# A two-layer streaming encoder: the depthwise convolution of its third mixer moved from taps on ScalarE and GpSimd to block-diagonal matmuls on TensorE

## The chip, the cores and the metric

The kernel runs on one core of a Trainium2 chip. The metric is the device time of one execution in microseconds (us). Before the change it is 3272.25 us, the median of three runs (3271.8 to 3272.7).

## The reference, cut to what matters

Two batches go through the same two layers: 1024 prompt tokens, and 32 sampled tokens with a cache of 2048 past keys. The model width is 1024. A layer is:

```python
h = rmsnorm(x, g_norm1[l]) * (1.0 + sc1) + sh1
z = h @ w_in[l]                      # 2116 columns, shared among three mixers
a_out = gmlp(za)     # gelu; v standardised in groups of 64 channels; 128x128 causal mixing; times u
b_out = sparse(...)  # indexer scores, the best 256 keys of each query kept, attention over them
c_out = conv(zc)
x = x + ga1 * (concatenate([a_out, b_out, c_out]) @ w_out[l])
h2 = rmsnorm(x, g_norm2[l]) * (1.0 + sc2) + sh2
x = x + ga2 * ((silu(h2 @ w_gate[l]) * (h2 @ w_up[l])) @ w_down[l])

def conv(zc):                        # 256 channels, 31 taps
    a, g = split(zc)
    hp = concatenate([state_or_zeros, a * sigmoid(g)])
    y[t, ch] = sum(hp[t + tap, ch] * w_dw[tap, ch] for tap in range(31)) + b_dw[ch]
    return silu(group_standardize(y, 4) * g_cn)
```

## The kernel before, in words

Everything is kept channel by partition: a tensor of 1024 channels is eight blocks of 128 partitions by 1056 tokens (1024 prompt, 32 sampled). The five engines run written-out programs in order and meet only at semaphores.

A weight strip is 1024 by 128. SP loads it into `w_raw` (L381), ScalarE rounds it to `w_hi` (`split_hi`, L579), GpSimd makes the rest `w_lo` (`split_lo`, L503), and TensorE does 72 matmuls of 352 columns with it (`strip`, L817): eight blocks of the input, three products each, three pieces of the tokens. Two triples of PSUM banks take turns; banks 6 and 7 are free for work beside the strips.

A layer begins with the norm. Then 17 input strips follow. VectorE rotates the queries and keys (`rotate`, L1221), four vector instructions per strip; ScalarE copies the others out. Beside strips 4 to 6 the indexer scores are made. Then the best 256 keys of each query are found by a bitwise threshold search of 31 rounds (`candidates` L1260, `decide` L1271). In one round VectorE counts three of the six score rows and ScalarE the other three (`count`, L621), and VectorE waits for ScalarE before it keeps or drops the bit. The rounds are spread over the strips by the table `SEARCH_AFTER`, and each engine runs them after its other work of that strip. In this order the convolution's and the gMLP's strips are the last eight (9 to 16). They do not fit in memory, so they are spilled to DRAM and read back.

After the strips comes a stretch that is called the gate here: gMLP's v is standardised, transposed, mixed by `w_spatial`, multiplied by u. Standardising is a mean matmul, `centre` (L1325), a squaring, a variance matmul, `deviation` (L636: logarithm and exponential) and `scale` (L1330). `finish_search` and the first `select` (L1303) run on VectorE beside it.

Then comes attention, for eight blocks i of 128 queries. TensorE makes the logits of block i+1 (`logits`, L975), then for each key block of block i the transposed scores (`st`, L991) and the product with the values (`pv`, L1008). VectorE takes maxima and writes the next `select`; ScalarE does the exponentials (`exponentials`, L719). A second search of 31 rounds, for the sampled tokens, runs in here too: some rounds in the maxima (`SEARCH_IN`), some beside the exponentials (`SEARCH_BESIDE`).

The convolution also runs here. For each of the 2 x 31 taps ScalarE multiplies the padded input `hp` by one weight per partition into `ctmp` (`tap`, L700) and GpSimd adds it to `cy` (L531). Its mean and variance follow after the sampled tokens' attention (L1088 to L1101), then SiLU, and the output projection of eight strips.

## Time and profile before

The profiled execution took 3274.92 us; its span, from the first to the last instruction, is 3273.0 us.

| stretch (us from the start) | what runs | length | TensorE busy |
|---|---|---|---|
| 0 to 140 | modulation weights, first norm, first strip | 140 | 88.1 |
| 140 to 401 | input strips of layer 0 | 261 | 229.8 |
| 401 to 437 | gate | 36 | 19.2 |
| 437 to 770 | attention and convolution | 333 | 257.1 |
| 770 to 870 | output projection | 100 | 95.3 |
| 870 to 1624 | feed-forward | 754 | 734.8 |
| 1624 to 3273 | layer 1, and the last norm | 1649 | 1449.9 |

The engines are busy 88% (TensorE), 50% (VectorE), 35% (ScalarE) and 25% (GpSimd) of the span. The table is a first guide only: an engine's busy share is an average over stages with different limits, so each stage is read by itself, above all by who waits for whom.

### The profile page before, as it was taken

What the parts mean: (1) busy time and instruction counts of PE and PEld (TensorE: products, weight loads), DVE (VectorE), ACT (ScalarE), POOL (GpSimd) and SP (SyncE); (2) the same over time, 40 slices, a digit from 0 to 9 for tenths busy, and PEclk for the clock granted to TensorE, in tenths of its full rate; (3) what the DMA queues carried; (4) which work ended last, traced back from release to release, by engine and by line L of the source; (5) the groups of instructions that cost most, each with busy time, mean ns of one, the idle gap of its engine ahead of it and who ended that gap; (6) DMA issues with size and microseconds to landing.
All of it is one profiled execution on the core that took longest, in us unless ns stands there. A gap on an engine that the chain in (4) does not pass through costs nothing.

```text
span 3273.0 us, 42010 instructions
## 1 busy us (share of the span) xinstructions
PE 2874.0 (88%) x15770; PEld 2472.4 (76%) x15770; DVE 1620.5 (50%) x2488; ACT 1139.7 (35%) x1338; POOL 815.1 (25%) x340
## 2 busy tenths in 40 slices
PE   6699576788799999999979966678889999999996
PEld 6679432238799999999967863223689999999996
DVE  7668667743433232433455875765324424333244
ACT  1327747733411111111242574684323111111113
POOL 0111127711122222222211102772011222222221
PEclk9999788899899999999989987899899999999998
DMA  9212200010122122222211230001011212222222
GB/s 350 85 40 75 103 2 0 1 33 26 45 92 72 63 89 69 83 77 71 78 59 50 69 116 2 0 1 33 20 52 71 84 64 81 67 96 68 74 82 79
DMA packets 70242, 214.49 MB, mean 66 GB/s; under 512 B 17280, under 2 KB 17536, under 8 KB 69120
## 3 DMA queue, kind: packets, MB, share of 16 engines
q1 hardware_dynamic: 67504, 202.71, 18.3%
q10 hardware_dynamic: 2640, 10.49, 0.8%
q8 instruction: 60, 0.98, 0.1%
q14 instruction: 38, 0.31, 0.0%
HBM read 196.76 MB, written 15.87 MB: 65 GB/s over the span
## 4 chain that ended last, share of the span: by engine, by line
PE 64%; DVE 14%; ACT 9%; issue 6%; DVEq 2%; DMA 2%; POOL 1%; ACTq 1%; SPq 0%; POOLq 0%
PE ps L825 56%; ACT notsel L626 4%; DVE smax L1443 2%; DMA w_ada<-in_w_ada 2%; PE ps L1015 1%; PE ps L854 1%; DVE s_keep L1274 1%; POOL cy L531 1%; PE ps L983 1%; DVE w_ada L1155 1%; DVE junk L1155 1%; ACT ctmp L710 1%; DVE notsel L1322 1%; DVE notsel L1319 1%; DVE score L1314 1%
## 5 line engine op out<-in xcount | busy, mean ns | idle before, releaser
L505 POOL TENSOR_TENSOR w_lo<-w_raw,w_hi 128x1024 fp32r<-128x1024 f32 x202 | 497.3, 2462 | 2184.8 <-ACT w_hi L586 2184.8
L825 PE MATMUL ps<-h_hi,w_hi 128*128 128x352 f32 x2928 | 648.2, 330 | 62.0 <-DVE h_lo L1143 48.4
L825 PE MATMUL ps<-h_lo,w_hi 128*128 128x352 f32 x2928 | 634.7, 325 | 0.0
L825 PE MATMUL ps<-h_hi,w_lo 128*128 128x352 f32 x2928 | 634.7, 324 | 0.0
L825 PEld LDWEIGHTS ps<-h_hi,w_hi 128*128 128x128 f32 x2928 | 499.6, 191 | 106.0 <-issue 78.1
L825 PEld LDWEIGHTS ps<-h_hi,w_lo 128*128 128x128 f32 x2928 | 505.7, 189 | 0.0
L825 PEld LDWEIGHTS ps<-h_lo,w_hi 128*128 128x128 f32 x2928 | 501.9, 189 | 0.0
L586 ACT CAST w_hi<-w_raw 128x1024 fp32r<-128x1024 f32 x202 | 211.3, 1046 | 642.5 <-PE ps L825 443.0
L531 POOL TENSOR_TENSOR cy<-cy,ctmp 128x1086 f32<-128x1086 f32 x120 | 303.5, 2529 | 229.2 <-ACT ctmp L710 224.4
L626 ACT ACTIVATE notsel<-score,s_cand 128x384 bf16<-128x384 f32 (+3 forms) x248 | 297.2, 1199 | 152.7 <-DVE s_cand L1262 152.5
L1547 DVE TENSOR_TENSOR act_f<-silu,ps 128x1056 f32<-128x1056 f32 x44 | 55.2, 1254 | 595.4 <-PE ps L825 595.4
L1530 DVE SCALAR_TENSOR_TENSOR x<-ps,mod,x 128x704 f32 (+2 forms) x240 | 125.4, 578 | 400.8 <-PE ps L825 394.8
L1155 DVE SCALAR_TENSOR_TENSOR junk<-w_ada,cond_row 128x1024 f32<-128x1024 f32 x124 | 243.7, 1965 | 33.3 <-issue 23.7
L825 PE MATMUL ps<-a_hi,w_hi 128*128 128x352 f32 x1056 | 227.8, 324 | 0.7 <-DVE x L1530 0.7
L825 PE MATMUL ps<-a_hi,w_lo 128*128 128x352 f32 x1056 | 227.5, 323 | 0.0
L825 PE MATMUL ps<-a_lo,w_hi 128*128 128x352 f32 x1056 | 227.0, 323 | 0.0
L794 ACT CAST a_hi<-act_f 128x1056 f32 x44 | 47.3, 1076 | 485.7 <-DVE act_f L1547 485.7
L1015 PE MATMUL ps<-probs,vaug 128*128 128x512 f32 x288 | 151.2, 655 | 70.9 <-ACT probs L724 70.9
L825 PEld LDWEIGHTS ps<-a_hi,w_lo 128*128 128x128 f32 x1056 | 180.8, 188 | 0.0
L825 PEld LDWEIGHTS ps<-a_hi,w_hi 128*128 128x128 f32 x1056 | 179.6, 189 | 1.3 <-issue 1.3
L825 PEld LDWEIGHTS ps<-a_lo,w_hi 128*128 128x128 f32 x1056 | 179.3, 188 | 0.0
L789 ACT ACTIVATE silu<-ps 128x1056 f32<-128x1056 f32 x44 | 46.4, 1055 | 379.6 <-PE ps L825 379.6
(222 smaller groups left out, 3301.7 us busy)
## 6 DMA issues: line engine op xcount, KB each, us to landing
w_ada<-in_w_ada SPq DMA_DIRECT2D x96, 512.0 KB, 5.1
w_raw<-in_w_up SPq DMA_DIRECT2D x88, 512.0 KB, 3.3
w_raw<-in_w_in SPq DMA_DIRECT2D x34, 512.0 KB, 3.6
w_ada<-in_w_ada SPq DMA_DIRECT2D x7, 2048.0 KB, 12.8
w_raw<-in_w_down SPq DMA_DIRECT2D x32, 384.0 KB, 3.1
w_ada<-in_w_ada ACTq DMA_DIRECT2D x5, 2048.0 KB, 12.5
w_raw<-in_w_down SPq DMA_DIRECT2D x32, 320.0 KB, 2.9
spill<-stage SPq DMA_DIRECT2D x16, 528.0 KB, 2.6
```

Of the source, the lines that this page charges most:

```text
L505: nc.gpsimd.tensor_tensor(w_lo[slot][:], w_raw[:], w_hi[slot][:].bitcast(F32), ALU.subtract)\
L531: nc.gpsimd.tensor_tensor(cy[:, m, :], cy[:, m, :], ctmp[t % 2][:], ALU.add)\
L586: nc.scalar.copy(w_hi[slot][:], w_raw[:]).then_inc(w_hi_ready.sem, 1)
L626: last = nc.scalar.activation(notsel[0:rows, SC_AT[n]:SC_AT[n + 1]], score[0:rows, SC_AT[n]:SC_AT[n + 1]], ACT.Sign, scale=-1.0, bias=s_ca ...
L789: nc.scalar.activation(as3(silu[:]), tiles3(0), ACT.Silu).then_inc(silu_ready.sem, 1)
L794: nc.scalar.copy(a_hi[:, f, :], act_f[:]).then_inc(a_hi_ready.sem, 1)
L825: last = nc.tensor.matmul(ps[:, bank + t, 0:TW], wt[slot][:, kk, :], mv[:, kk, t * TW:(t + 1) * TW], start=(kk == 0 and p == 0), stop=(kk ...
L1015: last = nc.tensor.matmul(ps[:, 2 + n, :], vaug[:, kb, n, :], probs[t % 2][:, n, :], start=(kb == 0), stop=(kb == i))
L1155: last = nc.vector.scalar_tensor_tensor(out=junk[:] if c == 0 else w, in0=w, scalar=1.0, in1=cond_row[:, c, :], op0=ALU.mult, op1=ALU.mult ...
L1443: nc.vector.tensor_reduce(smax[:, c // 512, :].rearrange("p (n b) -> p n b", n=2)[:, :, b], ps[:, bank:bank + 2, 0:w], AX.X, ALU.max).then ...
L1530: last = nc.vector.scalar_tensor_tensor(out=dst, in0=src, scalar=mod[:, which, d, c:c + 1], in1=dst, op0=ALU.mult, op1=ALU.add)
L1547: nc.vector.tensor_tensor(as3(act_f[:]), as3(silu[:]), tiles3(3), ALU.mult).then_inc(act_ready.sem, 1)
```

## The change

The input strips are put in another order: indexer first as before, then the convolution's four (a, gate, a, gate), gMLP's four, and only then k, v and the four q strips. Once the norm has read it, the residual x gives up its place in memory; in layer 1 it is first written to a DRAM buffer `xs`. Its place holds `hp`, gMLP's u and v, and the convolution's output, so nothing is spilled. x is read back (in layer 0 from the input) before the output projection, in two halves.

The convolution becomes matmuls. VectorE's 32x32 block transposes turn `hp` so that 32 consecutive tokens lie on the partitions of a 32-row block, four channels side by side. For each group of four channels, two 128x128 block-diagonal matrices of taps, made on the host, are multiplied with 34 columns. There are 128 such matmuls per layer, in 16 loads of 512 KB, four loads beside each of strips 8 to 11. VectorE adds the bias (`take_conv`) and turns the result back.

The five statistics groups (gMLP twice, all sampled tokens, convolution twice) run beside strips 12 to 16: the mean after block 1, the variance after block 6. The indexer scores of the sampled tokens, before spread over five strips, all run beside strip 7. The search starts after strip 6 with a new table of rounds.

```diff
+SAMPLE_IN = 7
+CONV_IN = {8: 0, 9: 4, 10: 8, 11: 12}
+CONV_LOADS, CONV_SLOTS = 16, 4
+STATS_IN = {12: 0, 13: 1, 14: 2, 15: 3, 16: 4}
+ST_GATE, ST_SAMPLED, ST_CONV = 0, 2, 3
+STAT_MEAN_AFTER, STAT_VAR_AFTER = 1, 6
...
-(S_KIW, S_QI0, S_QI1, S_K, S_V, S_Q0, S_Q1, S_Q2, S_Q3, S_CA0, S_CA1, S_CG0, S_CG1,
- S_AV0, S_AV1, S_AU0, S_AU1) = range(17)
+(S_KIW, S_QI0, S_QI1, S_CA0, S_CG0, S_CA1, S_CG1, S_AV0, S_AV1, S_AU0, S_AU1,
+ S_K, S_V, S_Q0, S_Q1, S_Q2, S_Q3) = range(17)
...
-SEARCH_AFTER = {S_Q1: 1, S_Q2: 2, S_Q3: 2, S_CA0: 3, S_CA1: 3, S_CG0: 3, S_CG1: 3, S_AV0: 3, S_AV1: 3, S_AU0: 3, S_AU1: 5}
...
+SEARCH_AFTER = {6: 1, 7: 2, 8: 3, 9: 3, 10: 3, 11: 3, 12: 4, 13: 3, 14: 3, 15: 3, 16: 3}
...
+        gv = place("gv", X_O, [P, 2, TOK], F32)
+        gu = place("gu", X_O + 2 * TILE, [P, 2, TOK], F32)
+        hp = place("hp", X_O + 4 * TILE, [P, 2, HPW], F32)
+        cy = place("cy", X_O + 4 * TILE, [P, 2, TOK], F32)
+        sg = place("sg", X_O + 4 * TILE + 2 * HPW * 4, [P, TOK], F32)
+        wsp = place("wsp", X_O + 5 * TILE + 2 * HPW * 4, [P, 4, P], F32)
...
+        hT = place("hT", R_O, [P, 2, HPB, CB], F32)
+        CW_O = R_O + 2 * HPW * 4
+        cw = [place(f"cw{s}", CW_O + s * 4096, [P, 8, P], F32) for s in range(CONV_SLOTS)]
+        kic = place("kic", CW_O + 8192, [P, PAST], F32)
...
+                if l:
+                    sp.dma_start(a["xs"], x[:]).then_inc(x_saved.sem, 16)
+                def load_conv(n):
+                    if n >= CONV_SLOTS:
+                        sp.wait_ge(cw_used.sem, cw_used.at(l, n - CONV_SLOTS + 1))
+                    sp.dma_start(cw[n % CONV_SLOTS][:], a["convw"][l, n]).then_inc(cw_loaded[n % CONV_SLOTS].sem, 16)
...
+                    if j == 7:
+                        for n in range(2):
+                            load_conv(n)
...
+                def bring_back(d):
+                    sp.dma_start(x[:, d, :], a["x"][:, d, :] if l == 0 else a["xs"][:, d, :]).then_inc(x_back[d // 4].sem, 16)
+                sp.wait_ge(gated.sem, gated.at(l, 2))
+                sp.wait_ge(av_stored.sem, av_stored.at(l, 16))
                 settle(sp)
...
+                for d in range(4):
+                    bring_back(d)
...
+                    if j == 1:
+                        sp.wait_ge(c_ready.sem, c_ready.at(l, 2))
+                        settle(sp)
+                        for d in range(4, KD):
+                            bring_back(d)
...
+                pool.wait_ge(h_ready.sem, h_ready.at(l, KD))
+                if l:
+                    pool.wait_ge(x_saved.sem, x_saved.at(l, 16))
+                nc.gpsimd.memset(hp[:, :, 0:HP0], 0.0)
+                nc.gpsimd.memset(hp[:, :, HP0 + SEQ:HPS - CW + 1], 0.0).then_inc(hp_edges.sem, 1)
...
+                    if j - 2 in (S_CG0, S_CG1):
+                        m = (S_CG0, S_CG1).index(j - 2)
+                        pool.wait_ge(z_act.sem, z_act.at(l, COPIED.index(j - 2) + 1))
+                        for dst, t0, n in ((HP0, 0, SEQ), (HPS, SEQ, DEC)):
+                            last = nc.gpsimd.tensor_tensor(hp[:, m, dst:dst + n], hp[:, m, dst:dst + n], sg[:, t0:t0 + n], ALU.mult)
+                        last.then_inc(hp_ready.sem, 1)
...
-                    for t in range(1, CW):
-                        pool.wait_ge(tap_ready.sem, tap_ready.at(l, CW * m + t + 1))
-                        nc.gpsimd.tensor_tensor(cy[:, m, :], cy[:, m, :], ctmp[t % 2][:], ALU.add)\
-                            .then_inc(tap_added.sem, 1)
...
-                def tap():
-                    m, t = taps.pop(0)
-                    wt = vec[:, V_WDW + CW * m + t:V_WDW + CW * m + t + 1]
-                    if t == 0:
-                        nc.scalar.activation(cy[:, m, :], hp[:, m, 0:CYW], ACT.Identity,
-                                             bias=vec[:, V_BDW + m:V_BDW + m + 1], scale=wt).then_inc(tap_ready.sem, 1)
...
-                    nc.scalar.mul(ctmp[t % 2][:], hp[:, m, t:t + CYW], wt).then_inc(tap_ready.sem, 1)
...
+                def convolve(n):
+                    m, group = n // 8, n // 2
+                    pe.wait_ge(cw_loaded[n % CONV_SLOTS].sem, cw_loaded[n % CONV_SLOTS].at(l, (n // CONV_SLOTS + 1) * 16))
+                    if n % 8 == 0:
+                        pe.wait_ge(hp_turned.sem, hp_turned.at(l, m + 1))
+                    if n == 0:
+                        pe.wait_ge(samp_taken.sem, samp_taken.at(l, 5))
+                    if n % 2 == 0 and group >= 2:
+                        pe.wait_ge(conv_taken.sem, conv_taken.at(l, group - 1))
+                    settle(pe)
+                    for c in range(4):
+                        at = 4 * (n % 2) + c
+                        for e in range(2):
+                            last = nc.tensor.matmul(ps[:, 6 + group % 2, at * (HPB - 1):(at + 1) * (HPB - 1)], cw[n % CONV_SLOTS][:, 2 * c + e, :],
+                                                    hT[:, m, e:e + HPB - 1, 4 * (n % 8) + c], start=(e == 0), stop=(e == 1))
+                    last.then_inc(cw_used.sem, 1)
...
+                def mean(s):
+                    if s == 0:
+                        pe.wait_ge(z_act.sem, z_act.at(l, COPIED.index(S_AV1) + 1))
+                        pe.wait_ge(conv_taken.sem, conv_taken.at(l, CONV_LOADS // 2))
+                    else:
+                        pe.wait_ge(st_rstd.sem, st_rstd.at(l, s))
+                    if s == ST_SAMPLED:
+                        pe.wait_ge(cy_ready.sem, cy_ready.at(l, 2))
+                    for src, _, out in stat_parts(s):
+                        last = average(out, src)
+                    last.then_inc(st_mean.sem, 1)
...
+                        if j == SAMPLE_IN:
+                            if 1 <= kk <= 5:
+                                sample_sum(kk - 1)
+                            if kk < 5:
+                                sample_dots(kk)
+                        if j in CONV_IN and kk % 2 == 0:
+                            convolve(CONV_IN[j] + kk // 2)
+                        if j in STATS_IN and kk == STAT_MEAN_AFTER:
+                            mean(STATS_IN[j])
+                        if j in STATS_IN and kk == STAT_VAR_AFTER:
+                            variance(STATS_IN[j])
...
+                def turn_input(m):
+                    dve.wait_ge(hp_ready.sem, hp_ready.at(l, m + 1))
+                    dve.wait_ge(state_loaded.sem, state_loaded.at(l, 32))
+                    nc.vector.transpose(hT[:, m, :, :], hp[:, m, :].rearrange("p (b c) -> p b c", c=CB)).then_inc(hp_turned.sem, 1)
+                def take_conv(group):
+                    dve.wait_ge(cw_used.sem, cw_used.at(l, 2 * group + 2))
+                    m, c = group // 4, 8 * (group % 4)
+                    made = ps[:, 6 + group % 2, 0:8 * (HPB - 1)].rearrange("p (c b) -> p c b", c=8)
+                    bias = vec[:, V_BDW + CB * m + c:V_BDW + CB * m + c + 8].unsqueeze(2)
+                    n = SEQ // CB
+                    nc.vector.tensor_tensor(co[:, 0:n, c:c + 8].rearrange("p b c -> p c b"), made[:, :, 0:n],
+                                            bias.to_broadcast([P, 8, n]), ALU.add)
+                    nc.vector.tensor_tensor(co[:, n:n + 1, c:c + 8].rearrange("p b c -> p c b"), made[:, :, n + 1:n + 2],
+                                            bias, ALU.add).then_inc(conv_taken.sem, 1)
+                    if group % 4 == 3:
+                        dve.drain()
+                        if m == 0:
+                            dve.wait_ge(hp_turned.sem, hp_turned.at(l, 2))
+                            dve.wait_ge(conv_stored.sem, conv_stored.at(l, 32))
+                        nc.vector.transpose(cy[:, m, :].rearrange("p (b c) -> p b c", c=CB), co[:]).then_inc(cy_ready.sem, 1)
...
+                    if j + 1 == SAMPLE_IN:
+                        for c, (c0, w) in enumerate(samp_chunks):
+                            dve.wait_ge(samp_sum.sem, samp_sum.at(l, c + 1))
+                            s0 = SC_AT[NSRCH - 1] + c0
+                            nc.vector.tensor_copy(score[0:DEC, s0:s0 + w], ps[0:DEC, 7, 0:w]).then_inc(samp_taken.sem, 1)
...
+                    if j in STATS_IN:
+                        scale(STATS_IN[j])
+                    if j + 1 in STATS_IN:
+                        dve.drain()
+                        centre(STATS_IN[j + 1])
+                    rounds = SEARCH_AFTER.get(j, 0)
+                    if j + 1 in CONV_IN:
+                        search(searched, 1)
+                        take_conv(CONV_IN[j + 1] // 2)
+                        search(searched + 1, 1)
+                        take_conv(CONV_IN[j + 1] // 2 + 1)
+                        searched, rounds = searched + 2, rounds - 2
+                    if rounds:
+                        search(searched, rounds)
+                        searched += rounds
...
+                for half in x_back:
+                    dve.wait_ge(half.sem, half.at(l, 4 * 16))
+                settle(dve)
```

## Rows read from the trace of the kernel before

**Rows 1.** Windows: busy time of each engine in a stretch (us, instructions), granted clock, DMA
```profile
1801.50:1965.30 163.80, 136.31 (x776) 123.41 (x774) 126.00 (x365) 110.32 (x212) 21.72 (x9) 0.93 0.26 92
1965.30:1996.40 31.10, 14.11 (x63) 11.19 (x64) 19.81 (x38) 12.86 (x16) 9.37 (x8) 0.72 0.02 4
1996.40:2074.90 78.50, 52.09 (x168) 19.02 (x168) 48.92 (x73) 40.22 (x38) 33.93 (x13) 0.78 0.00 0
2074.90:2290.60 215.70, 173.56 (x552) 61.62 (x552) 143.78 (x187) 143.29 (x136) 117.83 (x47) 0.93 0.05 13
2290.60:2329.60 39.00, 35.51 (x223) 24.18 (x222) 8.73 (x11) 7.60 (x8) 0.00 (x0) 0.78 0.00 1
2329.60:2341.80 12.20, 3.99 (x14) 2.19 (x13) 6.77 (x7) 11.22 (x13) 2.45 (x1) 0.84 0.03 4
```

**Rows 2.** Timeline, layer 1, end of the input strips: start, us, engine, line, operation [idle before]
```profile
1937.80 5.88 PE L914 MATMUL ps<-gv,con 128*128 128x352 f32 x12 [9.05 <-ACT stage L658]
1978.56 1.01 ACT L687 COPY vnat<-ps 128x1024 f32<-128x1024 f32 x1 [3.79 <-PE ps L941]
```

**Rows 3.** Chain that ended last, in order of time: start, us; output projection of layer 0
```profile
770.64 95.26 PE ps L825 x576
```

**Rows 4.** Timeline of VectorE, layer 1: threshold search and rotations beside the input strips
```profile
1801.51 0.48 DVE L1380 MEMSET score<- 64x64 f32 x6
1811.10 1.26 DVE L1224 TENSOR_TENSOR q<-ps,cossin 128x1056 f32<-128x1056 f32 x1
1833.63 1.26 DVE L1224 TENSOR_TENSOR q<-ps,cossin 128x1056 f32<-128x1056 f32 x1 [0.28 <-issue]
1834.82 1.38 DVE L1225 STREAM_SHUFFLE swapped<-ps 128x1056 f32<-128x1056 f32 x1
1838.79 0.67 DVE L1388 COPY score<-ps 32x512 f32<-32x512 f32 x1
1953.68 0.23 DVE L1262 TENSOR_SCALAR s_cand<-s_thr,s_bit 128x6 uint32<-128x6 uint32 x1 [0.41 <-issue]
1957.66 0.23 DVE L1262 TENSOR_SCALAR s_cand<-s_thr,s_bit 128x6 uint32<-128x6 uint32 x1 [0.41 <-issue]
```

**Rows 5.** Waits of TensorE in attention of layer 1: us in total, times, longest
```profile
PE ps L1015 <- ACT probs L724: 34.8, 18, 4.1
PE ps L983 <- DVE notsel L1322: 15.8, 3, 8.4
PE ps L983 <- DVE smax L1443: 14.4, 7, 3.3
```

**Rows 6.** Groups of instructions in attention of layer 1: busy, mean ns | idle before
```profile
L531 POOL TENSOR_TENSOR cy<-cy,ctmp 128x1086 f32<-128x1086 f32 x60 | 151.8, 2529 | 115.4 <-ACT ctmp L710 113.0
L710 ACT ACTIVATE ctmp<-hp,vec 128x1086 f32<-128x1086 f32 x60 | 70.5, 1192 | 21.1 <-POOL cy L531 20.9
L626 ACT ACTIVATE notsel<-score,s_cand 32x2080 bf16<-32x2080 f32 x31 | 62.6, 2020 | 29.5 <-DVE s_cand L1262 29.3
```

**Rows 7.** Timeline of TensorE, layer 1: the last block of queries and the sampled tokens
```profile
2273.76 1.13 PE L999 MATMUL ps<-q,k 64*128 64x512 f32 x4
2277.55 1.13 PE L999 MATMUL ps<-q,k 64*128 64x512 f32 x4
2320.78 1.95 PE L1085 MATMUL ps<-probs,vcache 128*128 128x128 f32 x16
```

**Rows 8.** Timeline of VectorE: the scan in a selection, without and beside GpSimd's additions
```profile
1998.74 1.23 DVE L1314 TENSOR_TENSOR_SCAN rank<-notsel 128x512 f32<-128x512 bf16 x1
2065.23 3.61 DVE L1314 TENSOR_TENSOR_SCAN score<-notsel 128x640 f32<-128x640 bf16 x1
```

**Rows 9.** Timeline of ScalarE, layer 1: ahead of the output projection
```profile
2331.50 0.38 ACT L714 ACTIVATE recip<-ps 64x256 f32<-64x256 f32 x1
2336.87 1.03 ACT L586 CAST w_hi<-w_raw 128x1024 fp32r<-128x1024 f32 x1
```

**Rows 10.** DMA issues of the first 100 us: KB each, median us to landing
```profile
x<-in_x SPq DMA_DIRECT2D x1, 4224.0 KB, 15.8
```

More of the change, by code:

```diff
@@ L283, in build @@
         z_act = signal("z_act", len(COPIED))
-        spilled = [signal(f"spilled{s}", 4 * DMA) for s in range(2)]
         wi_rows = signal("wi_rows", 1)
@@ L668, in _ @@
-                    if j == S_AU1:
-                        for m in range(2):
-                            square_centred(m, gv[:, m, :], mix[:, 4 + m, :])
+                    if j + 1 == SAMPLE_IN:
+                        for c in range(5):
+                            if c >= 1:
+                                act.wait_ge(samp_sum.sem, samp_sum.at(l, c))
+                            relu_step(N_DOTS + c, 1, samp_chunks[c][1])
+                    if j in STATS_IN:
+                        deviation(STATS_IN[j])
@@ L741, in _ @@
                     exponentials(t, P, PLACE["S", t], 512)
-                    for _ in range(2):
-                        if t >= 1 and taps:
-                            tap()
                     if kb == i:
                         reciprocals(i, t + 1, 2, 512)
-                assert searched == 2 * BITS and not taps
+                assert searched == 2 * BITS
                 for t, (c, w) in enumerate(SAMPLE_CHUNKS):
@@ new lines, in average, with variance @@
+                def average(out, src):
+                    if src.shape[2] == DEC:
+                        return nc.tensor.matmul(out, mean_w, src, start=True, stop=True)
+                    for half in range(2):
+                        last = nc.tensor.matmul(out[:, half, :], mean_w, src[:, half, :], start=True, stop=True)
+                    return last
+                def variance(s):
+                    pe.wait_ge(st_sq.sem, st_sq.at(l, s + 1))
+                    for _, tmp, out in stat_parts(s):
+                        last = average(out, tmp)
+                    last.then_inc(st_var.sem, 1)
@@ L926, in _ @@
[L926 to L932 removed]
+                pe.wait_ge(z_act.sem, z_act.at(l, len(COPIED)))
+                pe.wait_ge(z_rot.sem, z_rot.at(l, len(ROTATED)))
                 pe.wait_ge(wsp_masked.sem, wsp_masked.at(l, 1))
@@ L1087, in spv @@
                     last.then_inc(pv_used.sem, 1)
-                conv = [(2 + m, cy[:, m, :], ctmp[m], 5 * (1 - m), CYW) for m in range(2)]
                 for t in range(N_SS):
@@ L1277, in decide, with search @@
                     dve.drain()
+                def search(first, n):
+                    with dve.Fori(0, n) as b:
+                        candidates(0, PSRCH)
+                        decide(b + (first + 1), 0, PSRCH)
                 def finish_search(n0, n1):
@@ L1405, in _ @@
-                for m in range(2):
-                    scale(m, gv[:, m, :], mix[:, 4 + m, :])
                 finish_search(0, PSRCH)
-                dve.wait_ge(gu_loaded.sem, gu_loaded.at(l, 16))
+                assert searched == BITS
                 for m in range(2):
@@ L1617 @@
     bs = np.broadcast_to(bs, (DEPTH, 2, 2, HD, P)).reshape(DEPTH, 2, P, P).transpose(0, 2, 1, 3).reshape(DEPTH, P, 2 * P)
+    bdw = np.repeat(A["b_dw"].reshape(DEPTH, 2, 4, CB).transpose(0, 2, 1, 3).reshape(DEPTH, 4, 2 * CB), CB, 1)
     vec = np.concatenate([
-        by_part(A["g_norm1"]), by_part(A["g_norm2"]), by_part(A["b_ada"]), by_part(A["b_dw"]), by_part(A["g_cnorm"]),
-        A["w_dw"].transpose(0, 2, 1).reshape(DEPTH, 2, P, CW).transpose(0, 2, 1, 3).reshape(DEPTH, P, 2 * CW),
-        bs], 2)
+        by_part(A["g_norm1"]), by_part(A["g_norm2"]), by_part(A["b_ada"]), bdw, by_part(A["g_cnorm"]), bs], 2)
     assert vec.shape[2] == V_COLS
+    tap = np.arange(CB)[:, None] - np.arange(CB)[None, :] + np.array([-2, CW - 1])[:, None, None]
+    taps = np.where((tap >= 0) & (tap < CW), A["w_dw"][:, np.clip(tap, 0, CW - 1)].transpose(4, 0, 1, 2, 3), 0)
+    taps = taps.reshape(2, 4, 8, 4, DEPTH, 2, CB, CB)
+    convw = np.zeros((DEPTH, 2, 8, 4, CB, 4, 2, 4, CB), np.float32)
+    for b in range(4):
+        convw[:, :, :, b, :, :, :, b, :] = taps[:, b].transpose(3, 0, 1, 5, 2, 4, 6)
+    convw = convw.reshape(DEPTH, CONV_LOADS, P, 8, P)
     consts = np.zeros((P, C_COLS), np.float32)
```

396 lines of the change are left out of this document (168 added, 228 removed).

## The prediction

> **What bounds the kernel now.** I read the profile stage by stage. The table of stages shows where TensorE is not full: the input strips (261 us), the gate (36) and attention (333) of layer 0. Layer 1 repeats them within 4 us, so I work in layer 1 and double. The feed-forward and the output projection are full of matmuls, and the change leaves them alone.
>
> In the input strips the windows show TensorE busy 136.3 of 163.8 us from 1801.5 on [rows 1], so it is not what ends the stage. The timeline shows the statistics after the last strip at 1937.80, after a wait of 9 us, and the next real step (the copy of the transposed v) only at 1978.56 [rows 2]. What ends the stage is the threshold search. The reader is to see one round per 3.98 us on VectorE (1953.68 to 1957.66), in lockstep with ScalarE [rows 4]; 31 of them are 123.4 us. It is a serial chain, and everything that VectorE does between rounds makes it longer.
>
> In attention the waits of TensorE are 71.6 us, of which 65.0 are three rows: for exponentials 34.8, for the written selections 15.8, for maxima 14.4 [rows 5]. The groups say what stands in the way: ScalarE's 60 taps (70.5 us) and GpSimd's 60 additions (151.8 us) [rows 6]. The scan of 512 columns takes 1.23 us before the additions begin, and that of 640 takes 3.61 us beside them [rows 8]: VectorE is held up by GpSimd. Where no tap is left, one key block follows the other in 3.79 us without a wait (2273.76 to 2277.55) [rows 7]. The granted clock is 0.78 and 0.93 in the two windows of attention [rows 1], so part of the work ran at 1.2 GHz after waits.
>
> **The change, part by part, for one layer.**
>
> *Attention without taps: -53 us.* Taps and additions leave. Of the waits for exponentials (18, 34.8 us) the ones inside a block go: after the change a count of 2.02 [rows 6] and an exponential of 1.0 fit into the 3.79 of a key block, where before two taps of 1.19 came on top. One wait at the head of each block of queries stays (a search round lies ahead of the first exponential), 8 x 1.8 = 14. The waits for selections fall from 15.8 to 2, since a selection is some 6 us instead of 12 without GpSimd beside it [rows 8]. The waits for maxima stay at 12 of 14.4, because the rounds inside the maxima still go back and forth. With 3 us of small ones 31 stay, and 40.6 go. The clock: at c of full speed a share 2(1-c) of the time ran at half speed, 0.44 and 0.14. If fewer waits bring that to 0.2 and 0.04, half of the difference on 52.1 and 173.6 us of matmuls is 6 + 9 = 15 [rows 1]. That is 55.6; I take 53, since some of the clock's gain is in the waits already. Bounds: 25 (only the waits that stand behind two taps) and 80 (all waits and the clock).
>
> *Gate: -12.6.* The statistics are gone from it, and so are the sigmoid, a table load and the reading back. TensorE can transpose v while the last rounds run. From the copy at 1978.56 [rows 2] to the first logits at 1996.4 are 17.8 us; the copy can start 0.7 us after the search, so 31.1 becomes 18.5. VectorE's end of the search (6.7 us) hides behind the copy and the mixing matmuls, as before. Bounds 8 and 16.
>
> *Sampled tokens and the way to the output projection: -9.* 24 matmuls for the convolution's statistics go (7.7 us of the 39.0 and 12.2) [rows 1], and ScalarE's four passes for the deviations between 2331.50 and 2336.87 [rows 9]. What is late next is ScalarE's split of the first mixer blocks. Bounds 6 and 11.
>
> *Input strips: +46.* This is where the work goes. TensorE has room: eight strips take 95.26 us [rows 3], 11.9 each, while VectorE and ScalarE need 12 to 21 us per strip. So the search chain is what I sum. Before, from 1801.5: 9.6 for the start of the search (to 1811.10), 123.4 for the rounds, three rotations of 5.16 (1833.63 to 1838.79), 15.5 [rows 4]; 3.1 for the sampled scores; 12.2 for two centrings and waits. That is 163.8.
> After:
> - start and rounds 9.6 + 123.4.
> - The strips of k and all four q now come in the search: five rotations, 25.8.
> - The sampled scores all lie beside strip 7. TensorE waits there for VectorE's start of the search, then VectorE for five steps of 1.5 + 1.4 us: 9.7.
> - Statistics on VectorE: five centrings and five scalings, eight of them of 1024 columns at about 1.26 (the first row of a rotation) [rows 4], two small: 10.8.
> - Convolution on VectorE: 16 small additions, 0.65 a pair, 5.2, and four block transposes. No row has one. The nearest is the shuffle of the same size, 1.38 [rows 4]; I take that, 5.5. Bounds 4 and 12.
> - Waits 20: ScalarE's copy and split ahead of the first round in strips 7 to 10 (7 together), its squares ahead of a round (5 x 1), its deviation in strip 12, which has no rotation to hide it (4), and take_conv for TensorE's second pair of loads in strips 8 and 9 (4).
>
> The sum is 210, so +46. Bounds 30 (half the waits, cheap transposes) and 66 (every added wait seen).
>
> *TensorE's share.* 128 matmuls of 34 columns, each with its own weights, have no row. The nearest is 16 of 128 columns with new weights each in 1.95 us, 0.122 each [rows 7]. That makes 15.6 us, 3.9 per strip in four strips: 15.8 us per strip, against 14 to 15 of VectorE there, so nearly hidden. Below it can't go by more than the columns: nothing to 15.6 us. Above, 0.24 would add some 12 us to the chain.
> The Trainium skill, page "SBUF — State Buffer", section "Door 1: The DMA port swizzle", states that SBUF is read in 16-byte lines and an access that crosses to a new line pays a penalty. The columns of `hT` lie 128 bytes apart, so each is on another line. No row here has such a read, and the page gives no time; by 0.122 the sum stands, and rival B is what a penalty large enough would do.
>
> *x out and back: 0.* Writing x in layer 1 is 4224 KB; x came in within 15.8 us [rows 10], and the norm's 30 us cover it. Ahead of it in SP's queue are vec and cossin, behind it strip 1, needed only when the norm is over. GpSimd's memset waits for it, with the split of strip 2 queued behind; if x took over 35 us, TensorE would wait for that. The way back is two halves of 8 us. The first has all of attention. The second starts about 3 us into the output projection, with the third strip's weights behind it; these are needed 11.9 us in [rows 3]. If that cover fails, it costs up to 10 us per layer.
>
> **The sum.** 46 - 12.6 - 53 - 9 = -28.6 per layer, -57 for two. From the profiled 3274.92 that is 3218; the median is 2.7 lower, so 3215.
>
> **The rivals.**
> *A, slower: lockstep of the statistics.* In strips 12 to 16 the mean can't start before ScalarE's deviation of the strip before, and the variance waits for VectorE's centring. TensorE so halts in every strip and restarts at 1.2 GHz. If the rest of a strip after the mean (7 blocks, 10 us at full clock, 20 at half) outlasts VectorE's rounds, the next rotation waits. The price is up to 8 us in each of five strips. It decides from 28.6 / 5 = 5.7 us per strip. With 8, and 45 in attention, a layer is +46 + 40 - 12.6 - 45 - 9 = +19: 3311. For it: the clock of 0.72 in the gate [rows 1] shows what waits do. Against it: rounds, rotation and scaling are 21 us per strip, longer than even the slow rest.
> *B, slower: conv matmuls slow.* At 0.35 us each, 29 us more per layer, break-even; at 0.45 it gives 3299.
> *C, no change: attention is search-bound.* If the 31 sampled rounds set the pace, only 25 us go: 46 - 12.6 - 25 - 9 = -0.6, 3271. Against it: 3.1 us per round against 3.79 of a key block.
> *D, better: waits hidden.* Strips +32, attention -65: -54.6 per layer, 3163.
>
> **How the numbers follow.** My forecast 0.64 (its own range 3190 to 3245), A 0.10, B 0.04, C 0.07, D 0.15. Two tenths of a per cent, 6.5 us, is what a measurement tells from no change. Slower takes A, B and a little of C: 0.14. Same is most of C: 0.06. Faster is the rest, 0.80. The range goes from near D to where A begins: 3168 to 3264.
>
> **What would show it.** In the profile after: from the start of the search to its end about 210 us instead of 164 in each layer; first logits 18 to 19 us after the last round; the scans in attention at 1.5 to 2.3 us instead of 3.6 to 4.0; key blocks 3.8 us apart from the second on; attention about 270 us with the sampled tokens; no wait for x in the output projection. Wrong if a transpose takes over 4 us, if the strips grow by over 75 us, or if attention shrinks by less than 30.

## The result

The changed kernel takes 3241.2 us (median of 4 runs, 3240.5 to 3243.4), the kernel before, run beside it, 3272.0: a ratio of 0.9907, with a 95% interval from 0.9889 to 0.9924, 30.8 us less. The forecast was 3215 within 3168 to 3264. The direction is right and the time lies in the range, but only about half of the expected gain came. Later runs were not made beside the changed kernel but beside the kernel before, which came out at 3272.0 to 3274.1 each time, so "below the changed kernel" always means below this 3241.2. The profiled execution took 3241.9 us, its span 3239.5.

In the rows PE is TensorE, PEld its weight loads, DVE VectorE, ACT ScalarE and POOL GpSimd. Layer 1 in four stages: length, busy time of TensorE, its weight loads, VectorE, ScalarE and GpSimd, granted clock, DMA share, GB/s. Set them against [rows 1].
```profile
1787.10:2012.60 225.50, 178.67 (x1049) 157.81 (x1047) 151.78 (x405) 120.65 (x226) 24.01 (x11) 0.90 0.18 60
2012.60:2031.50 18.90, 13.14 (x54) 10.32 (x55) 16.35 (x36) 3.94 (x9) 3.35 (x2) 0.81 0.00 1
2031.50:2267.00 235.50, 206.71 (x715) 77.38 (x716) 137.73 (x260) 114.88 (x112) 0.00 (x0) 0.94 0.07 21
2267.00:2309.00 42.00, 33.63 (x215) 23.01 (x213) 9.03 (x12) 10.96 (x13) 2.35 (x1) 0.77 0.00 0
```
The first is the input strips from the start of the search, the second the gate, the third the blocks of queries (before: two windows, 78.5 and 215.7), the fourth the sampled tokens and the way to the output projection, whose first matmul is here:
```profile
2310.11 1.22 PE L840 MATMUL ps<-m_hi,w_hi 128*128 128x352 f32 x3 [6.28 <-DVE m_lo L1595]
```

| layer 1, us | before | after | difference | forecast |
|---|---|---|---|---|
| input strips, from the start of the search | 163.8 | 225.5 | +61.7 | +46 |
| gate | 31.1 | 18.9 | -12.2 | -12.6 |
| blocks of queries | 294.2 | 235.5 | -58.7 | -53 |
| sampled tokens, way to the projection | 51.2 | 43.1 | -8.1 | -9 |
| sum | | | -17.3 | -28.6 |

Three of four terms are within 6 us. The one that failed is the strips, by 15.7 us a layer. Outside the four stages a block transpose of 1.3 us now stands ahead of the search. At the start of the output projections the new kernel is 16.7 us ahead in layer 0 (753.93 against 770.64 [rows 3]) and 31.7 in layer 1 (2310.11 against 2341.8 [rows 1]), so layer 1 itself gives 15: the 17.3 of the table, less that transpose and 1 us that lies between the projection of layer 0 and the search. Layer 0 is like layer 1 in the kernel before, more than the table of stages shows: its first logits start at 428.8, not at 437, 31 us after its last round.

The waits of VectorE in the strips of layer 1 (us in total, times, longest), after:
```profile
DVE co L1399 <- PE ps L908: 22.7, 6, 5.3
DVE s_keep L1317 <- ACT notsel L661: 17.6, 30, 2.4
DVE score L1465 <- PE ps L891: 10.1, 4, 4.1
DVE gv L1383 <- ACT st_tmp L681: 3.6, 1, 3.6
DVE gv L1377 <- PE ps L930: 2.2, 1, 2.2
```
and of before, the row that answers to the second:
```profile
DVE s_keep L1274 <- ACT notsel L626: 14.0, 31, 2.4
```
With the last of the 31 rounds, which ends just behind this window, the second row is 17.8. The first row is the finding: `take_conv` waits 22.7 us for the convolution's matmuls, where the forecast had 4. Two of these waits on VectorE's timeline (the bracket is the idle time ahead of the copy), then TensorE with one load's matmuls between two blocks of a strip, then the group:
```profile
1839.12 0.63 DVE L1399 TENSOR_TENSOR co<-ps,vec 128x256 f32<-128x256 f32 x1 [2.67 <-PE ps L908]
1848.51 0.63 DVE L1399 TENSOR_TENSOR co<-ps,vec 128x256 f32<-128x256 f32 x1 [5.29 <-PE ps L908]
...
1849.30 1.28 DVE L1408 STREAM_TRANSPOSE cy<-co 128x1056 f32<-128x1056 f32 x1 [0.16 <-issue]
```
```profile
1870.06 1.88 PE L908 MATMUL ps<-hT,cw 128*128 128x34 f32 x16
1871.76 0.73 PE L840 MATMUL ps<-h_hi,w_hi 128*128 128x352 f32 x3
```
```profile
L908 PE MATMUL ps<-hT,cw 128*128 128x34 f32 x256 | 30.1, 282 | 0.0
```
A load has 8 matmuls in the program and 16 records in the trace; the layer's 128 have 256. From the start of a load's matmuls to the strip's next one are 1.70 us (1870.06 to 1871.76), 0.213 each, which is 27 us of TensorE a layer instead of 15.6. (The 30.1 us of the group are the lengths of the records, and neighbours overlap.)

The same count read again in the row from which the price was taken: the `x16` of L1085 in [rows 7] belongs to a loop over four key blocks and two heads, which is 8 matmuls, each recorded twice. 1.95 us is 0.244 each, not 0.122; measured as above, from their start to the next matmul (1.88 us, to 2322.66), it is 0.235. The strips' matmuls, whose parts were rounded to fp32r, have one record each (576 for eight strips of 72 [rows 3]), and the rows call both kinds f32, so only the program's own count tells them apart.

### The profile page after: what moved, and what is told of

Read it like the earlier page. It is cut to its first block, busy times and chain, and to the rows that moved or that the text cites. A ratio compares the mean times of both kernels' runs of the same rounds, so it can differ in the third digit from the quotient of the medians.

```text
span 3239.5 us, 42719 instructions
## 1 busy us (share of the span) xinstructions
PE 2912.6 (90%) x16266; PEld 2529.4 (78%) x16266; DVE 1535.8 (47%) x2536; ACT 1000.3 (31%) x1228; POOL 512.0 (16%) x222
## 4 chain that ended last, share of the span: by engine, by line
PE 74%; DVE 10%; ACT 7%; issue 4%; DVEq 2%; DMA 2%; ACTq 0%; POOL 0%; SPq 0%; POOLq 0%
PE ps L840 60%; PE ps L1067 4%; ACT notsel L661 4%; PE ps L1051 2%; PE ps L908 2%; DVE smax L1525 2%; DMA w_ada<-in_w_ada 2%; PE ps L869 1%; DVE junk L1198 1%; PE ps L1055 1%; DVE w_ada L1198 1%; PE ps L1057 1%; PE ps L1137 1%; ACT hf L609 0%; DVE xn L1183 0%
## 5 line engine op out<-in xcount | busy, mean ns | idle before, releaser
L840 PE MATMUL ps<-h_hi,w_hi 128*128 128x352 f32 x2928 | 660.9, 334 | 62.3 <-DVE h_lo L1186 48.8
L1067 PE MATMUL ps<-probs,vaug 128*128 128x512 f32 x288 | 141.1, 622 | 31.8 <-ACT probs L755 31.8
L1276 DVE TENSOR_SCALAR_CACHE_REDUCE notsel<-score,s_cand 128x512 bf16<-128x512 f32 x186 | 153.8, 877 | 7.3 <-issue 0.4
```

The costliest lines, as they stand in the source:

```text
L840: last = nc.tensor.matmul(ps[:, bank + t, 0:TW], wt[slot][:, kk, :], mv[:, kk, t * TW:(t + 1) * TW], start=(kk == 0 and p == 0), stop=(kk ...
L1067: last = nc.tensor.matmul(ps[:, 2 + n, :], vaug[:, kb, n, :], probs[t % 2][:, n, :], start=(kb == 0), stop=(kb == i))
L1276: nc.vector.tensor_scalar(notsel[0:rows, SC_AT[n]:SC_AT[n + 1]], score[0:rows, SC_AT[n]:SC_AT[n + 1]], scalar, None, compare, ALU.add, acc ...
```

## The experiments

All times are medians, with the kernel before beside each (3272.5 to 3274.1 us); "search" is the time from the sign of the first threshold (1792.9) to VectorE's first step after the last round (2012.8), 219.9 us in layer 1 of the changed kernel.

### Half of the convolution's matmuls, and the same matmuls on neighbouring columns

`e1_half_taps`:
```
-                        for e in range(2):
+                        for e in range(1):
     ... hT[:, m, e:e + HPB - 1, 4 * (n % 8) + c], start=True, stop=True)
```


> The changed kernel with only the first of the two matmuls per channel (64 convolution matmuls a layer instead of 128), every wait and copy as it was; half of the convolution is left out. Theory 1 (the input strips are longer than forecast because VectorE's copies wait for TensorE's convolution matmuls, 22.7 us a layer, each matmul costing 0.21 us instead of 0.12): 64 x 0.21 = 13.7 us less on TensorE in strips 8 to 11, of which 11 to 13 leave the search chain of each layer: 3241 becomes 3215 to 3219, and the wait of the copies falls below 11 us. Rival (the copies are late because ScalarE's copies and splits hold the strips back, the matmuls have room): under 4 us a layer, 3233 or more, and the wait stays near 20.

Measured: 3214.1 us (3211.5 to 3216.8, 4 runs), ratio to before 0.9818 (0.9801 to 0.9834), 27 us below the changed kernel. Search 205.9 instead of 219.9. The time is 1 us below what theory 1 gave, since more than the 13 us left the chain. VectorE's waits in the strips:
```profile
DVE score L1465 <- PE ps L891: 10.1, 4, 4.1
DVE co L1399 <- PE ps L908: 8.2, 5, 3.5
```
A load's matmuls now take 0.81 us from start to start instead of 1.70, which is 14.2 us a layer less. The wait of the copies falls by 14.5 us and the search by 14.0: TensorE's added matmuls lay on the search chain with nearly their whole length.

`e2_side_by_side`:
```
-     hT[:, m, e:e + HPB - 1, 4 * (n % 8) + c]
+     hT[:, m, :, :].rearrange("p b c -> p (b c)")
+         [:, 32 * (n % 8) + c + e:32 * (n % 8) + c + e + HPB - 1]
```


> The changed kernel with the same 128 convolution matmuls, but their 34 moving columns lie side by side in memory instead of 128 bytes apart; so they multiply other data, and the convolution's values are left out. Theory 1a (a matmul costs what its 128x128 weights cost to load and pass): no change, 3241 within 4, and a pair of loads still takes 3.4 us of TensorE. Rival B of the prediction (the strided read costs): the price falls from 0.21 to 0.12 each, 12 us less on TensorE per layer, 3219.

Measured: 3243.5 us (3242.2 to 3244.1, 4 runs), ratio to before 0.9908 (0.9892 to 0.9925), search 219.9: no change. The groups for both layers, with the columns side by side, then in the changed kernel 128 bytes apart:
```profile
L908 PE MATMUL ps<-hT,cw 128*128 128x34 f32 x512 | 59.9, 272 | 0.0
```
```profile
L908 PE MATMUL ps<-hT,cw 128*128 128x34 f32 x512 | 60.2, 282 | 0.0
```
From its start to the next matmul a load takes 1.70 us in both. Rival B's mechanism is out: the stride, and with it the penalty that the prediction weighed, costs nothing that can be measured here. What is left is the price of a matmul with weights of its own: 34 columns here cost 0.213 us and 128 columns 0.235 in [rows 7], so the number of columns hardly matters. That the weight loads set it is argued from this and was not tried by itself. The Trainium skill, page "TensorE: Matmul & The Clock Gate", section "LDWEIGHTS (loading the stationary operand)", says that a load takes a time that goes with the 128 columns of the weights, by its formula 107 ns. An estimate from that page for the two recorded passes is 0.213 us; the trace agrees in the spacing, 0.213 from one matmul to the next, while each load's own record is 192 ns long and overlaps its neighbours.

### Search rounds moved to where VectorE waits

`e3_rounds_earlier`:
```
-SEARCH_AFTER = {6: 1, 7: 2, 8: 3, 9: 3, 10: 3, 11: 3, 12: 4, 13: 3, 14: 3, 15: 3, 16: 3}
+SEARCH_AFTER = {6: 1, 7: 3, 8: 4, 9: 4, 10: 4, 11: 3, 12: 3, 13: 2, 14: 2, 15: 2, 16: 3}
...
-                        search(searched + 1, 1)
+                        search(searched + 1, 2)
                         take_conv(CONV_IN[j + 1] // 2 + 1)
```


> The changed kernel, all of the computation kept, with search rounds moved from strips 12 to 15 into the strips 7 to 10, where VectorE waits for the convolution: one more round after each, placed ahead of the second copy. Theory 1: VectorE's waits there (22.7 us a layer) are filled by four rounds of 3.98 us, and strips 12 to 16 have room for fewer rounds, so 12 to 16 us leave the chain of each layer: 3209 to 3217. Rival (rival A of the prediction: in strips 12 to 16 the statistics run in lockstep with TensorE, so fewer rounds there only uncover their waits): under 4 us a layer, 3233 or more, and the first instruction of a rotation waits for TensorE.

Measured: 3205.3 us (3202.8 to 3209.4, 4 runs), ratio to before 0.9795 (0.9779 to 0.9812), 36 us below the changed kernel and 4 below the range of theory 1. Search 203.5 instead of 219.9, which is 33 of the 36 us for two layers. Another 4 lie behind the search of layer 1 (293.2 us from the last round to the projection instead of 297.3); their cause is not shown. The copies' wait:
```profile
DVE co L1399 <- PE ps L908: 6.9, 6, 2.7
```
15.8 of 22.7 us are filled, and the chain is shorter by 16.4. Theory 1 holds. The lockstep of rival A is there as a pattern: in the changed kernel TensorE waits 22.3 us in strips 12 to 16 for ScalarE's deviation, but no rotation waits for TensorE, and fewer rounds there made the kernel faster.
```profile
PE ps L930 <- ACT st_tmp L681: 14.7, 3, 8.4
PE ps L928 <- ACT st_tmp L681: 7.6, 1, 7.6
```
A second set of runs, beside `e7_waits_filled`:

> The kernel with the rounds moved into strips 7 to 10 once more, beside the next one on the same chip: 3205 within 5.

Measured: 3206.6 us (3204.6 to 3209.2, 4 runs), ratio 0.9794 (0.9779 to 0.9809).

### Statistics of an eighth of the size

`e6_small_statistics`:
```
-            src = gv[:, s - ST_GATE, 0:SEQ] if s < ST_SAMPLED else cy[:, s - ST_CONV, 0:SEQ]
+            src = gv[:, s - ST_GATE, 0:128] if s < ST_SAMPLED else cy[:, s - ST_CONV, 0:128]
```
(and `st_tmp` and the banks alike).

> The changed kernel with the statistics of 1024 columns (two for the gate, two for the convolution) cut to 128 columns each: every step and wait stays, the work is an eighth; most columns stay without their statistics. Theory 1 (the search chain is a sum of what VectorE does): eight centrings and scalings of 1.2 us become 0.2, and ScalarE's squares and TensorE's averages ahead of them shrink, so 12 to 16 us leave each layer's strips: 3209 to 3217. Rival A (the price is the lockstep, each mean behind the deviation before it): the steps are all still there, and under 6 us a layer go, 3229 or more.

Measured: 3215.9 us (3214.4 to 3221.2, 4 runs), ratio to before 0.9825 (0.9809 to 0.9841), 25 us below the changed kernel. Search 207.4, 12.5 less. A centring of a prompt part takes 0.29 us here instead of 1.22:
```profile
1944.52 0.29 DVE L1377 TENSOR_TENSOR cy<-cy,ps 128x128 f32<-128x128 f32 x1
```
The time is as theory 1 had it, and rival A is out: all the steps were still there. But VectorE's own work is only half of the 12.5 us. Its centrings and scalings of prompt parts shrink by 5.9 us in all (one scaling still took 1.90, beside GpSimd's split). The other 6.6 are its waits for the engines whose work shrank too: for ScalarE's half of a round 14.9 instead of 17.8, for the deviation of strip 12 2.1 instead of 3.6, for the mean none instead of 2.2.

### What the taps had cost attention

Buffers of their own, work of the taps' size. `e4_additions` (GpSimd) and `e5_scalings` (ScalarE); `e8_both` has both (shortened: the engine's waits for its own last step are left out):
```
+                for t in range(60):                    # e4, GpSimd, ahead of its next split
+                    nc.gpsimd.tensor_tensor(dacc[:], dacc[:], dsrc[:], ALU.add)
...
                     exponentials(t, P, PLACE["S", t], 512)
+                    for _ in range(2):                 # e5, ScalarE, 62 in all
+                        if t >= 1 and taps:
+                            nc.scalar.mul(dtmp[n % 2][:], dsrc[:], 1.5)
```


> The changed kernel, all kept, with 60 additions of 128x1086 on GpSimd put into each layer's attention (buffers of their own, one after the other from its start), as the convolution had them before; no scalings on ScalarE. Theory 2a (of the 53 us of the forecast for attention a large part came from GpSimd holding VectorE up: scans of 3.61 us, late selections): 15 to 25 us more per layer, 3271 to 3291, and the scans of 640 columns are back over 3 us. Theory 2b (it was ScalarE's taps that kept the exponentials late): under 6 us more per layer, below 3253.

> The changed kernel, all kept, with 62 scalings of 128x1086 on ScalarE put into each layer's attention where the taps stood before, and no additions on GpSimd. Theory 2b (taps kept the exponentials late, 40 us of waits): 25 to 40 us more per layer, 3291 to 3321, and TensorE's waits for the exponentials go back above 30 us. Theory 2a: under 10 us per layer, below 3261, since a count, two scalings and an exponential (5.4 us) could otherwise hide in other waits.

> The changed kernel, all kept, with both dummies in each attention, the 60 additions on GpSimd and the 62 scalings on ScalarE, not waiting for each other. Theory (the attention term of the forecast, 53 us a layer, is what these two cost): 3241 + 106 = 3347, between 3325 and 3365. Rival (part of the gain came from elsewhere, the sampled tokens' own steps or the statistics that left the gate): 3321 or less.

| | us (range) | ratio to before (95%) | from first logits to the projection, layer 1 |
|---|---|---|---|
| before | 3272.0 | 1 | 345.4 |
| changed | 3241.2 | 0.9907 | 278.6 |
| additions | 3379.6 (3375.1 to 3381.0) | 1.0323 (1.0306 to 1.0341) | 320.7 |
| scalings | 3266.7 (3264.3 to 3268.7) | 0.9980 (0.9970 to 0.9989) | 289.0 |
| both | 3388.4 (3386.3 to 3389.0) | 1.0354 (1.0337 to 1.0372) | 321.6 |

The additions cost 42 us in that stage and the scalings 10. So my theory 2b, on which some 21 us of the forecast's term for attention rest (the waits for exponentials, from 34.8 to 14), fell: ScalarE's time for the taps is the small part. Theory 2a had the cause, but no total came in its range either: the scalings end 6 us above its 3261. Unbound, the additions start with the gate, where none ran before, and the gate grows from 18.7 to 42.1 us. That is why the totals of `e4` and `e8` miss the expectations by so much, and they can't be compared with the kernel before. It also means that only 48 of the 60 additions lie in the stage of the table. The windows from the first logits on, with VectorE's busy time third, for the additions and then for the scalings:
```profile
2123.10:2443.80 320.70, 248.41 (x916) 102.86 (x928) 201.02 (x273) 127.22 (x126) 130.32 (x48) 0.85 0.05 15
```
```profile
2046.60:2335.50 288.90, 245.09 (x916) 100.50 (x928) 147.81 (x273) 187.14 (x188) 2.35 (x1) 0.90 0.05 17
```
VectorE has the same 273 instructions in both, for 201 us and for 148. Five of its steps, in `e4_additions` (turning the scores in the gate; the spread of the maxima; the maxima themselves; keeping a bit in the second search; comparing scores in a selection):
```profile
2084.61 15.93 DVE L1313 TENSOR_SCALAR score<-score,s_sgn 128x384 f32<-128x384 f32 x6
...
L1549 DVE SCALAR_TENSOR_TENSOR negmax<-con,smax 128x1024 fp32r<-128x1024 f32 x8 | 17.1, 2137 | 5.0 <-PE ps L1069 4.4
L1537 DVE TENSOR_REDUCE smax<-ps 128x2 f32<-128x1024 f32 x24 | 29.0, 1224 | 8.0 <-PE ps L1051 7.0
L1329 DVE TENSOR_TENSOR s_keep<-s_cnt,s_need 128x1 uint32<-128x1 f32 x31 | 22.1, 714 | 28.2 <-ACT notsel L673 27.5
L1372 DVE TENSOR_SCALAR_CACHE_REDUCE score<-score,s_tmp 128x640 f32<-128x640 f32 x1 | 0.9, 879 | 0.1
```
and the same five in the changed kernel:
```profile
2016.40 3.06 DVE L1301 TENSOR_SCALAR score<-score,s_sgn 128x384 f32<-128x384 f32 x6
...
L1537 DVE SCALAR_TENSOR_TENSOR negmax<-con,smax 128x1024 fp32r<-128x1024 f32 x8 | 9.8, 1226 | 6.0 <-PE ps L1057 5.6
L1525 DVE TENSOR_REDUCE smax<-ps 128x2 f32<-128x1024 f32 x24 | 29.0, 1224 | 16.2 <-PE ps L1039 15.3
L1317 DVE TENSOR_TENSOR s_keep<-s_cnt,s_need 128x1 uint32<-128x1 f32 x31 | 4.9, 158 | 29.8 <-ACT notsel L661 29.2
L1360 DVE TENSOR_SCALAR_CACHE_REDUCE score<-score,s_tmp 128x640 f32<-128x640 f32 x1 | 0.9, 878 | 0.1
```
The reading of PSUM is not held up, and of the steps that read SBUF not all are. Keeping a bit and spreading the maxima take two inputs from SBUF and take 4.5 and 1.7 times as long. The first is tiny, but it stands 31 times in the serial second search and alone makes up 17 of the 53 us. Turning the scores has one input and is held up too; comparing them has one input and is not (879 ns against 878). The Trainium skill, page "GPSIMD Engine Reference", section "8. Key points", says that GpSimd shares its SBUF interfaces with VectorE and contends with instructions in a two-port mode or with two SBUF inputs. The trace agrees for the steps with two inputs (714 ns against 158, 2137 against 1226) and for a step with one that stays free (879 against 878). Whether turning the scores ran in a two-port mode, no row says.

What was left open is the wait for exponentials, 34.8 us before [rows 5]. `e4` gave 19.3, `e5` 20.0, `e8` 22.9. So the two were bound to each other as the taps had been:
```
+    act.wait_ge(dummy_added.sem, dummy_added.at(l, n))          # scaling n: addition n-2
+    pool.wait_ge(dummy_scaled.sem, dummy_scaled.at(l, t + 1))   # addition t: scaling t
```


> The changed kernel, all kept, with 60 scalings on ScalarE and 60 additions on GpSimd in each attention, bound to each other as the taps were: an addition waits for its scaling, a scaling for the addition two before it, and the first ones wait for the second selection. Theory 2c (the waits for exponentials came neither from the scalings' time nor from GpSimd's alone, but from ScalarE standing behind GpSimd in that chain): TensorE's waits for the exponentials go from 16.6 back to 30 or more per layer, where 62 free scalings gave 20.0 and both unbound 22.9, the gate stays at 18.7, and attention with the sampled tokens grows by 50 to 60 us per layer: 3341 to 3361. Rival (it is only GpSimd's hold on VectorE, which the unbound additions showed with 43 to 45 us in attention): 3321 to 3333, exponentials under 25.

Measured: 3372.8 us (3368.0 to 3373.4, 4 runs), ratio 1.0300 (1.0284 to 1.0315). Gate 19.1, then 339.9 us to the projection, 61.3 more than without, of the 66.8 that the change took out of this stage. The total is above the range that I gave: 66 us a layer are added where 50 to 60 were expected. Of the 132 us, 65 lie in layer 0 and 62 in layer 1 between the last round and the projection, and 5 outside. TensorE's waits there, then ScalarE's for GpSimd:
```profile
PE ps L1098 <- ACT probs L769: 30.7, 17, 3.6
PE ps L1066 <- DVE notsel L1402: 20.3, 4, 8.5
PE ps L1066 <- DVE smax L1556: 17.6, 7, 3.8
```
```profile
ACT dum L778 <- POOL dum L582: 25.4, 20, 2.4
```
The pattern of before is back: 17 waits for exponentials against 18, and ScalarE waits 25.4 us for GpSimd, as it waited 20.9 inside the taps, which stood in [rows 6] all along. The 19 us more than in `e4` are not all from the coupling. Here all 60 additions lie in the stage, not 48, and VectorE is busy for 209.4 us instead of 201.0; the waits for exponentials are 30.7 instead of 19.3. No run separates the two.

### Filling the waits that are left

On top of the moved rounds. `e7_waits_filled`: two rounds among the sampled copies of strip 7, TensorE's steps for them spread over eight blocks, and one round ahead of the first scaling in strip 12 (the rounds come from the same or the neighbouring strip). `e10_strip_12`: the last of these alone.
```
+                            if c in (1, 3):            # e7, among the sampled copies
+                                search(searched, 1)
...
+                    if j == 12:                        # e7 and e10
+                        search(searched, 1)
                     if j in STATS_IN:
                         scale(STATS_IN[j])
```


> The kernel with the rounds moved into strips 7 to 10, all of the computation kept, and two more waits of VectorE filled with rounds: one round ahead of the first scaling in strip 12 (which waits 3.6 us for ScalarE's deviation and 2.2 for the mean), and two rounds among the five sampled copies beside strip 7 (10.1 us of waits for TensorE), whose TensorE steps are spread over eight blocks instead of six. Theory 1 (the chain is a sum, and each wait filled by a round shortens it): 5 to 9 us less per layer than with the rounds moved alone: 3187 to 3195. Rival (TensorE's strips 7 to 11 now end last, since the copies wait 6.9 us for it still, and a later strip 7 pushes them on): within 4 of 3205.

> The kernel with the rounds moved into strips 7 to 10, all of the computation kept, and one round of strip 12 put ahead of the first scaling on VectorE and ahead of the deviation on ScalarE; the sampled copies as they were. Theory 1: the 5.8 us of waits in strip 12 (3.6 for the deviation, 2.2 for the mean before it) are partly covered: 2 to 4 us less per layer, 3198 to 3202. Rival (the next mean and TensorE's strip only come later by the same): 3204 to 3208.

Measured: 3210.9 us (3207.5 to 3212.5, 5 runs) and 3209.1 (3206.4 to 3215.2, 5 runs), ratios 0.9807 (0.9794 to 0.9820) and 0.9809 (0.9796 to 0.9823). Neither beats the 3205 to 3207 of the moved rounds alone. In `e7` the sampled copies wait less and the convolution's copies more (11.3 against 7.0):
```profile
DVE co L1410 <- PE ps L919: 11.3, 6, 5.3
DVE score L1476 <- PE ps L902: 7.1, 4, 3.0
```
Theory 1 fell in both, and both came out 1 to 2 us above what even the rivals allowed, which is less than their runs scatter. In `e7` the search is 206.0 us against 203.5, and the mechanism is the rival's: a later strip 7 moves TensorE's next strips on, and the copies wait for them. In `e10` the search is 204.3 against 203.5: of the 5.8 us of waits in strip 12, 4.3 are still there, and the next rotation now waits 0.9 us for TensorE. The version with the moved rounds beats both kernels, by 67 us the one before and by 35 the changed one.

## Why the prediction was right, and where it was wrong

- **Bound by the search chain in the strips.** Right. `e3` took 15.8 us of waits out of it and the chain fell by 16.4.
- **Input strips, +46; it was +61.7.** The term that failed, though 61.7 lies within its bounds (30 to 66). Its parts: the wait of `take_conv` 22.7 instead of 4 (+18.7); the sampled copies 13.0 instead of 9.7 (+3.3); waits in strip 12 5.8 instead of 4 (+1.8); ScalarE late for a round 3.8 more than before (17.8 against 14.0), where 12 were expected for copies and squares (-8.2); only three of the four transposes in the stage (-1.6). Together +14.0 of 15.7; the rest I haven't located. Rotations (25.6 us, forecast 25.8), statistics (10.8) and transposes (1.28 to 1.35 each, forecast 1.38) were right.
- **The step that was wrong** is the price of a convolution matmul, 0.122 us, from a row whose 16 records are 8 matmuls. With 0.24, I wrote, some 12 us would come onto the chain. It was 0.213, and the 0.091 more are 11.6 us of TensorE for 128 matmuls; `e1` shows that such time lies on the chain nearly whole. So the price makes up some 12 of the 15.7. The wait of the copies was also taken too low by itself: in `e1` the matmuls take 13.0 us a layer, less than the 15.6 of the forecast, and the copies still wait 8.2 us instead of 4.
- **Gate, -12.6.** Right: -12.2, and 18.9 us after the last round as forecast.
- **Attention, -53.** The size was right (-58.7), the reasons in part. The waits left over are 31.3 us against the 31 forecast:
```profile
PE ps L1067 <- ACT probs L755: 16.6, 7, 3.5
PE ps L1035 <- DVE smax L1525: 11.4, 7, 4.1
PE ps L1035 <- DVE mix L1501: 2.5, 1, 2.5
```
  Scans take 1.49 to 2.29 us and key blocks follow in 3.78, both as forecast:
```profile
2087.09 1.49 DVE L1363 TENSOR_TENSOR_SCAN score<-notsel 128x640 f32<-128x640 bf16 x1
2185.85 2.29 DVE L1363 TENSOR_TENSOR_SCAN score<-notsel 128x1024 f32<-128x1024 bf16 x1
```
```profile
2244.36 1.13 PE L1051 MATMUL ps<-q,k 64*128 64x512 f32 x4
2248.14 1.13 PE L1051 MATMUL ps<-q,k 64*128 64x512 f32 x4
```
  TensorE's busy time in the blocks of queries fell from 225.7 us (52.1 + 173.6 [rows 1]) to 206.7 for the same matmuls, 19 us where 15 were put down to the clock; with 40.3 us of waits less (71.6 to 31.3) that is the gain. That the clock gave the 19 is what the granted clock suggests (0.94 in this stage after, 0.78 and 0.93 in its two parts before [rows 1]); no run tried it alone. But "two taps of 1.19 came on top" put the waits for exponentials down to ScalarE's own time. That time is worth 10 us (`e5`); 42 come with GpSimd's additions, which hold VectorE up (`e4`); bound together they are 61 (`e9`) of the 66.8 that left attention and the sampled tokens. So that the size came out is in part luck: half of the waits were taken away for a reason that is the small part. Rival C is out: attention gave 58.7, not 25.
- **Sampled tokens and the way on, -9.** Right: -8.1.
- **x out and back, 0.** Right for the time, but not without a wait. VectorE stands idle for 3.07 us at the place where the program waits for x (3.46 in layer 0, 0.17 ahead of the same step before the change); the transfers of the second half were issued up to 2316.0.
```profile
2314.87 4.76 DVE L1595 TENSOR_TENSOR m_lo<-mix,m_hi 128x1056 fp32r<-128x1056 f32 x4 [1.41 <-ACT m_hi L787]
2322.71 0.94 DVE L1611 MEMSET sumsq<- 128x1056 f32 x1 [3.07 <-issue]
2324.14 1.57 DVE L1604 SCALAR_TENSOR_TENSOR x<-ps,mod,x 128x704 f32 x3 [0.49 <-issue]
```
  ScalarE's split of the third strip waits 5.7 us for the weights queued behind x. TensorE waits for neither: behind the first matmul of the projection no wait of it is recorded in the eight strips, in either layer. Nor does the way out show: from 1560 us to the search TensorE waits 11.8 and 8.8 us for VectorE, before it was 12.2 and 8.8. A kernel without the transfers wasn't tried.
- **The sum.** The four terms give -17.3 a layer instead of -28.6. The time lies in the range because the range was wide, and because attention gave 5.7 us a layer more than forecast, which hid a third of the miss in the strips.

## What to carry to other kernels

Before a price per instruction is taken from a group's count, count the instructions of that group in the code: fp32 matmuls with 128x128 weights are two records each here, and the factor of two cost some 12 of the 28.6 us a layer that I had forecast. Where a serial chain sets the end, look for the waits that a new step puts into it, and move pieces of the chain into them; here moving four rounds gave more (36 us) than the change did (31). Work on GpSimd that looks free can cost the steps of VectorE beside it, the small ones of a serial chain above all: read the duration of the same VectorE instruction with and without it, and look for an engine that waits for GpSimd in a chain of small steps.

## What the hardware showed that I hadn't expected

- A fp32 matmul of 34 columns with its own 128x128 weights takes 0.213 us, with 128 columns 0.235; a step of 128 bytes between the columns changes nothing (1.70 us for eight either way).
- With GpSimd adding 128x1086 fp32 without a pause, VectorE's in-place scaling of the scores takes 15.93 us instead of 3.06 for six, five times as long, a comparison of 128x1 values from SBUF 714 ns instead of 158, while its reductions from PSUM (1224 ns) and a TENSOR_SCALAR_CACHE_REDUCE with one input from SBUF (879 ns) take what they took.
- A 32x32 block transpose of 128x1056 fp32 takes 1.28 us, less than the shuffle of the same size (1.38 [rows 4]).
